# Summing the rows of the modulation matrix on GpSimd instead of VectorE during attention

## The reference

```python
def first_block(x, c, positions, ada_w, ada_b, ...):
    c_act = jax.nn.silu(c)
    mod = jnp.matmul(c_act, ada_w[l]) + ada_b[l]         # ada_w: 1024 x 6144
    sh1, sc1, gt1, sh2, sc2, gt2 = [m[:, None, :] for m in jnp.split(mod, 6, axis=-1)]
    h = rmsnorm(x, norm1_g[l]) * (1.0 + sc1) + sh1
    ...                                                  # projections
    out_fox = forgetting_attention(fq, fk, fv, log_f)
    out_dsa = dsa_attention(dq, dk, dv, iq, ik, iw)
    ...
    x = x + gt1 * jnp.matmul(merged, w_out[l])
    h2 = rmsnorm(x, norm2_g[l]) * (1.0 + sc2) + sh2
    y = hierarchical_moe(h2, ...)
    x = x + gt2 * y
```

## Time and profile before

| | us |
|---|---|
| median of 3 runs | 3842.69 (3840.71 to 3844.96) |
| the profiled execution | 3842.19 |
| its span in the profile | 3840.4 |
| VectorE busy | 2073.3 (54%) |
| GpSimd busy | 1007.2 (26%) |
| ScalarE busy | 1391.9 (36%) |

### The profile page before, as it was taken

The page is one execution under the profiler, slowest core; times in us unless marked ns, Lnnn a source line. Parts: engine busy times, 40 slices in busy tenths (PEclk is TensorE's granted clock), DMA queues, the critical chain, the costliest instruction groups (busy, mean ns, idle before and its releaser), DMA issues. The chain is left out here.

```text
span 3840.4 us, 46493 instructions
## 1 busy us (share of the span) xinstructions
PE 3280.3 (85%) x15172; PEld 2573.2 (67%) x15172; DVE 2073.3 (54%) x2675; ACT 1391.9 (36%) x1802; POOL 1007.2 (26%) x532
## 2 busy tenths in 40 slices
PE   5977888678889559999966999979879999999868
PEld 4745665445567348888744888867658788787747
DVE  6257886578652569988855544343353123133263
ACT  3144554456620358878842055210221000000141
POOL 1311322000024021111102444344233333343322
PEclk8999998789999879999988999989999999999979
DMA  5201221133024179999982122132221111111222
GB/s 210 59 23 44 76 71 27 36 108 108 9 94 141 63 280 398 399 399 399 398 313 83 44 82 87 41 99 80 79 71 49 44 49 49 44 49 44 77 77 109
DMA packets 349339, 471.47 MB, mean 123 GB/s; under 512 B 31359, under 2 KB 227901, under 8 KB 348229
## 3 DMA queue, kind: packets, MB, share of 16 engines
q1 hardware_dynamic: 332852, 414.28, 31.2%
q0 software_dynamic: 9872, 34.09, 2.2%
q10 hardware_dynamic: 6528, 22.02, 1.7%
HBM read 402.10 MB, written 62.98 MB: 121 GB/s over the span
## 5 line engine op out<-in xcount | busy, mean ns | idle before, releaser
L399 PE MATMUL acc<-Ah,whi 128*128 128x512 f32 x2376 | 947.4, 399 | 140.4 <-ACTq L829 38.2
L373 POOL TENSOR_TENSOR whi<-wraw,one 128x1024 fp32r<-128x1024 f32 (+3 forms) x216 | 394.1, 1825 | 2074.9 <-PE acc L401 1590.9
L400 PE MATMUL acc<-Al,whi 128*128 128x512 f32 x2376 | 934.7, 393 | 0.0
L401 PE MATMUL acc<-Ah,wlo 128*128 128x512 f32 x2376 | 933.8, 393 | 0.0
L399 PEld LDWEIGHTS acc<-Ah,whi 128*128 128x128 f32 x2376 | 450.8, 190 | 255.2 <-issue 87.5
L400 PEld LDWEIGHTS acc<-Al,whi 128*128 128x128 f32 x2376 | 450.8, 190 | 100.0 <-issue 4.4
L401 PEld LDWEIGHTS acc<-Ah,wlo 128*128 128x128 f32 x2376 | 449.7, 189 | 97.6
L375 POOL TENSOR_TENSOR wlo<-wraw,whi 128x1024 fp32r<-128x1024 f32 (+3 forms) x216 | 506.8, 2346 | 16.9
L1710 DVE TENSOR_TENSOR mlo<-mraw,mhi 128x1024 fp32r<-128x1024 f32 x256 | 305.5, 1221 | 51.4 <-ACT mhi L1660 42.8
L1660 ACT ACTIVATE mhi<-mraw 128x1024 fp32r<-128x1024 f32 x256 | 266.1, 1065 | 96.3 <-DMA mraw<-in_exp_w 59.1
L399 PE MATMUL acc<-Bh,whi 128*128 128x512 f32 x640 | 254.3, 397 | 26.2 <-DVEq L2202 17.6
(11 more groups left out here) (421 smaller groups left out, 4889.8 us busy)
## 6 DMA issues: line engine op xcount, KB each, us to landing
mraw<-in_exp_w SPq DMA_DIRECT2D x512, 256.0 KB, 10.8
mraw<-in_exp_w SPq DMA_DIRECT2D x128, 512.0 KB, 12.1
wraw<-in_w_in SPq DMA_DIRECT2D x72, 512.0 KB, 3.8
wraw<-in_w_up SPq DMA_DIRECT2D x48, 512.0 KB, 3.8
gates<-TT ACTq DMA_DIRECT2D x32, 512.0 KB, 2.6
TT<-in_ada_w SPq DMA_DIRECT2D x32, 512.0 KB, 3.9
TT<-gates SPq DMA_DIRECT2D x32, 512.0 KB, 4.5
wraw<-in_w_down SPq DMA_DIRECT2D x24, 512.0 KB, 3.7
```

What stands on the lines that cost most here:

```text
L373: ch(pool.tensor_tensor(whi[:, r, 0:k, 0:m], wraw[:, r, 0:k, 0:m], one[:, 0:1].unsqueeze(2).broadcast_to([P, k, m]), ALU.mult))
L399: pe.matmul(o, whi[:, r, j, 0:m], ih[:, k0 + j, cols], start=(j == 0), stop=False)
L400: pe.matmul(o, whi[:, r, j, 0:m], il[:, k0 + j, cols], start=False, stop=False)
L401: last = pe.matmul(o, wlo[:, r, j, 0:m], ih[:, k0 + j, cols], start=False, stop=(j == k - 1))
```

## The change

The 32 tile steps of the four quarters are taken out of VectorE's `ada` and become a loop of their own on GpSimd. GpSimd has no single instruction here for multiply-and-add: for k = 0 one multiply writes the sum, for k > 0 the tile is multiplied in place by the scalar of its partition (stretched over 1024 columns) and then added to the sum. VectorE keeps the addition of `ada_b`. The order among tiles isn't tied to attention's units any more but by semaphores alone: a tile's landing, and, for quarters 2 and 3, `ada_cols`, since these reuse the sums' buffers. The loads of SyncE are unchanged. The first two sixths stay on VectorE.

```diff
--- before.py
+++ after.py
@@ -1133,11 +1133,6 @@
         def ada(n):
 
             q, k = n // KD, n % KD
-            if 0 <= q < 4:
-                dve.wait_ge(S("ada2_land%d" % (n % 2)), 16 * (n // 2 + 1))
-                ada_rows(dve, ch, TT[:, 2 + q % 2, :], TT[:, n % 2, :], k)
-                if k == KD - 1:
-                    dve.sem_inc(S("ada_sum"), 1)
             q -= 1
             if k == 3 and 0 <= q < 4:
                 dve.wait_ge(S("ada_cols"), q + 3)
@@ -1162,6 +1157,25 @@
                 rotate(dve, ch, QKD[:, 8 + j, :], TT[:, 3, :], TT[:, 2, :])
                 dve.sem_inc(S("q_roped"), 1)
             ada(u - NB)
+
+    @block.gpsimd
+    def _(pool):
+        ch = chain(pool, "pool")
+        for n in range(4 * KD):
+            q, k = n // KD, n % KD
+            total, rows = TT[:, 2 + q % 2, :], TT[:, n % 2, :]
+            pool.wait_ge(S("ada2_land%d" % (n % 2)), 16 * (n // 2 + 1))
+            if k == 0 and q >= 2:
+                pool.wait_ge(S("ada_cols"), q + 1)
+            scale = cact[:, 1, k:k + 1].broadcast_to([P, T])
+            if k == 0:
+                ch(pool.tensor_tensor(total, rows, scale, ALU.mult))
+            else:
+                ch(pool.tensor_tensor(rows, rows, scale, ALU.mult))
+                ch(pool.tensor_tensor(total, total, rows, ALU.add))
+            pool.sem_inc(S("ada_used"), 1)
+            if k == KD - 1:
+                pool.sem_inc(S("ada_sum"), 1)
 
     @block.scalar
     def _(act):
```

## The result

| | before | after |
|---|---|---|
| median of 4 runs, us | 3841.7 (3840.6 to 3845.0) | 3864.4 (3861.9 to 3870.1) |
| profiled execution, its span | 3842.2, 3840.4 | 3863.0, 3861.3 |
| first to last bias pass of attention, us | 316.4 | 339.0 |

The change makes the kernel slower, by 22.7 us: the ratio is 1.006, with a 95% interval of 1.0045 to 1.0075. The forecast was 3868.7 us, +26.0, with a range of 3850 to 3900.

The account below looks back on a forecast made before the run. VectorE was taken to bound attention units with rows. From 3842.7 us, removing the rows gave -22.4 us and VectorE's stalls beside GpSimd +48.4 us, net +26.0, so 3868.7 us, range 3850 to 3900 us.

Parts of the forecast that it names:

- What bounds the stage: Attention rounds with modulation rows: VectorE sets the pace, busy 31.65 of 39.49 us, and a row is on the path.
- The gain, 22.4 us: Rows leaving VectorE in four attention rounds: 4 x (39.5 - 33.9) = 22.4 us is all that can be won.
- The stalls: VectorE's scaling passes wait for whole GpSimd passes: 1.8 us between a unit's scalings; bias passes cost nothing extra.
- the four projection splits: GpSimd work already falling into attention; beside it scaling passes of 0.75 us alone took 1.15 and 1.34 us.
- Passes in a unit: Attention under GpSimd's rows: 2.8 passes and 6.5 us a unit, 21.4 units, each 2.26 us above free pace: +48.4 us.
- GpSimd's own pace: GpSimd's row loop: multiplies and adds stretched to 2.4 to 3 us, rows at 4.6 us each.
- Waits that move: GpSimd hardly waits for loads; its wait before quarters 2 and 3 delays nothing urgent; sums cost TensorE little.
- No stalls: Rival: scalings pass GpSimd, attention runs at 4.24 us a unit and the gain comes in; 3825 us, chance 0.06.
- The bite is half: Rival: loads or TensorE's waits leave GpSimd idle where scalings come; stalls 24 us, 3844 us, chance 0.08.
- the third rival: TensorE's clock falls in attention, shown by a granted clock under 0.8; +57 us, 3899 us, chance 0.12.

Follow-up runs that it names:

- narrow passes: The changed kernel with every GpSimd pass cut from 1024 to 8 columns, loads, waits and semaphores kept: 3822.8 us (0.9947).
- the other form: The changed kernel with VectorE's scaling passes of units 8 to 39 also writing out a sum nobody reads: 3825.8 us (0.9958).
- passes of half length: The changed kernel with every GpSimd pass cut in two halves of 512 columns, all work kept, 120 passes: 3841.4 us (0.9996).

## Why the prediction was right, point by point

- **What bounds the stage.** Right: VectorE was on the path in units with rows. The same 18.6 us of longer scaling passes cost 18.9 us there and 1.9 us once the rows were gone.
- **The gain, 22.4 us.** The mechanism was right and the size 3.0 us too high: 19.4 us. The step that failed took one dsa round with rows (39.5 us) and dsa rounds without (33.9 us) for all four rounds. Three of the four are of the fox kind. They took 47.3, 39.8 and 39.3 us before, and 39.4, 35.2 and 38.0 us with narrow passes; the dsa round took 39.5 and 33.5. It could have been seen: the first of them was 8 us longer than the round in the earlier trace rows.
- **The stalls.** The rows on the four projection splits named the right VectorE line, and the earlier trace rows rightly cleared the bias pass. The second scaling of a unit stalls 1.5 us in the mean (34.3 / 23), where the sum had 1.7 (1.8 for the pause before it); the first 1.0, where the sum had 1.1 to 1.2 in the mean over the widths.
- **Passes in a unit.** The sum had 2.8 passes and 6.5 us a unit over 21.4 units. Measured 60 / 23 = 2.6 passes and 143.4 / 23 = 6.2 us. The two errors offset one another: 23 x (6.2 - 4.24) = 45 us against 48.4. By the run with narrow passes the loss is 41.3 us; about 3 us of the rest is the pace of the item on the gain.
- **GpSimd's own pace.** Wrong in a small way: I expected its passes stretched to 2.4 to 3 us. They stay at 1.89 and 2.37 us. It looks as if a scaling pass of 0.5 us fits largely into the changeover between two passes (0.18 us, and the last and first tenths of the records beside it); no run varies that. So rows took 143.4 / 32 = 4.48 us each, not 4.6. For a two-input pass of this size the Trainium skill (GPSIMD Engine Reference, Elementwise — side-by-side cycle accounting) gives 2.6 cycles an element, by which 2.22 us is an estimate. The trace shows 1.89 for the multiply and 2.37 for the add.
- **Waits that move.** As forecast they cost nothing: the longest row wait for a load is 2.1 us, the wait for the old sum's columns 0.9 us, and TensorE never waits for a sum in the changed kernel.
- **The rivals.** "No stalls" would have needed the scaling passes to go unhindered; with the other form they did, and the gain came in. That 3825.8 us is so near that rival's 3825 is luck, since its gain was 3 us too high and its 5 us for TensorE's wait for a sum aren't there. "The bite is half" didn't come true: GpSimd waits for loads only 5.1 us in all. The kernel with passes of half length comes near its number (3841.4 against 3844) in another way, with 37.0 us of stalls where that rival had 24. TensorE's clock did fall, to 0.86 and 0.76 in the two windows, from 0.91. By the sign that the prediction gave (under 0.8) the third rival would hold in the second of them, but its 3899 us didn't come. A slower TensorE can delay VectorE only where VectorE waits for it, 7.2 us in the whole stretch, or for ScalarE behind it, 1.5 us; no run separates a cost of the clock within that.

In sum, attention loses 339.0 - 316.4 = 22.6 us, which is -18.7 (narrow passes against the kernel before) and +41.3 (the change against narrow passes). In the medians it is -19.4 and +41.6, +22.2 us, against the +22.7 measured. The forecast had -22.4 and +48.4. The mechanism was right, but that the total came within 3.3 us is in part luck: the gain was 3 us too high and the price 7 us too high, and the two errors offset each other.

## What to carry to other kernels

Before work goes to GpSimd, list the VectorE instructions that run beside it by their inputs: in these runs those in the fast SBUF-to-SBUF form, or with two inputs in SBUF, waited for up to a whole GpSimd pass, and one such line in a tight loop cost more than the removed work had. If it must be there, give it a form with one input at normal rate, which lost 0.3 us here and saved up to 2, or cut the GpSimd passes short. Look for one place in the old trace where the two engines already meet; here it gave the mechanism, and the size within 4 us, helped by two errors that offset each other.

## What the runs showed of the hardware that I had not expected

- In these stretches VectorE pays nearly all of the exclusion: 57.1 us of stalls on its side, and about 4 us on GpSimd's (60 passes at 130.2 us in all, against 32 x 1.89 + 28 x 2.35 = 126.3).
- The same multiply on VectorE at 1024 columns, 0.75 us alone, took up to 2.65 us beside GpSimd (2.69 at 768 columns); in the slower form it took 1.28 us at most. The nominally slower form was the faster by far.
- The loss isn't proportional to GpSimd's time: 70 to 73 us of passes cost 3.5 and 6.1 us of attention (6.7 and 10.1 us in the medians), 130 us of passes cost 41.3. The first 0.3 to 0.7 us of stall in a unit cost next to nothing.
